# Five modulation blocks moved out of the weight ring of a fused two-block transformer kernel

## The reference, cut to what matters

```python
for l in range(DEPTH):                      # first block, DEPTH = 2, x is 256 x 1024
    x = layer_norm(ALPHA * x + 0.5 * swiglu(x, ffn_w1[l, 0], ffn_w2[l, 0]), ...)
    x = layer_norm(ALPHA * x + hybrid_mixer(x, ...), ...)
    x = layer_norm(ALPHA * x + 0.5 * swiglu(x, ffn_w1[l, 1], ffn_w2[l, 1]), ...)

def adaln(cond, w_mod, b_mod):              # second block, for c and c_ctx
    m = silu(cond) @ w_mod + b_mod          # 1024 x 3072 a layer
    return split(m)                         # shift, scale, gain
...
for layer in range(DEPTH):
    h = rms_norm(x, g_pre) * (1 + scale) + shift        # latent and context rows
    y = even_mixer(h) if layer == 0 else odd_mixer(h)
    x = x + gain * rms_norm(y, g_post)
```

## Time and profile before

| | |
|---|---|
| median of 3 runs | 2401.09 us (2400.11 to 2401.63) |
| the profiled execution | 2397.17 us, span 2395.4 us |
| mean granted TensorE clock | 0.975 |
| PE busy | 94% (2252.9 us) |
| DVE busy | 59% |
| ACT busy | 37% |
| mean busy share of 16 DMA engines by q1 | 38.1% |

### The profile page before, as it was taken

One profiled execution on the slowest core, in us unless ns is written; L12 is line 12 of the kernel. 1 busy time (PEld: TensorE's weight loads), 2 busy tenths in 40 slices (PEclk: granted clock), 3 DMA queues, 4 the chain that ended last, 5 costly groups with the idle time before them and its releaser, 6 DMA issues.

```text
span 2395.4 us, 34326 instructions
## 1 busy us (share of the span) xinstructions
PE 2252.9 (94%) x14514; PEld 1966.8 (82%) x14514; DVE 1409.0 (59%) x2025; ACT 878.2 (37%) x993; POOL 10.5 (0%) x23
## 2 busy tenths in 40 slices
PE   7997999899979979999998989999999998999988
PEld 7985999699869959998897658888777757999966
DVE  5554876655455547766655546665655348565663
ACT  4432364143324323552432242222334242343432
POOL 0000000000000000000000000000000000000000
PEclk9998999999989989999999999999999998999998
DMA  6454555455454545555554511111101242232321
GB/s 257 181 205 164 192 196 181 171 197 208 176 193 178 208 166 189 193 182 206 200 208 151 193 71 70 71 71 71 71 36 71 79 175 72 80 132 76 137 106 53
DMA packets 26552, 349.39 MB, mean 146 GB/s; under 512 B 2912, under 2 KB 3168, under 8 KB 5728
## 3 DMA queue, kind: packets, MB, share of 16 engines
q1 hardware_dynamic: 23888, 336.49, 38.1%
q0 software_dynamic: 2512, 10.72, 1.3%
HBM read 346.14 MB, written 1.05 MB: 145 GB/s over the span
## 4 chain that ended last, share of the span: by engine, by line
PE 85%; DVE 6%; ACT 3%; DMA 3%; DVEq 1%; issue 1%; ACTq 1%; SPq 0%
PE banks L695 12%; PE banks L700 12%; PE banks L696 12%; PE banks L778 10%; PE banks L854 8%; PE banks L916 5%; PE banks L912 5%; PE banks L913 5%; DMA ring<-weights 2%; PE banks L737 2%; PE banks L1091 2%; PE banks L1092 2%; DVE w_lo L1784 2%; PE banks L1089 2%; PE banks L930 2%; PE banks L926 2%
## 5 line engine op out<-in xcount | busy, mean ns | idle before, releaser
L1784 DVE TENSOR_TENSOR w_lo<-ring,w_hi 128x2048 fp32r<-128x2048 f32 x290 | 662.5, 2291 | 537.3 <-ACT w_hi L1294 533.9
L1294 ACT ACTIVATE w_hi<-ring 128x2048 fp32r<-128x2048 f32 x290 | 554.8, 1916 | 766.7 <-PE banks L700 476.7
L695 PE MATMUL banks<-x_hi,w_hi 128*128 128x256 f32 x2208 | 515.0, 276 | 1.4 <-ACT arena L1388 1.4
L696 PE MATMUL banks<-x_lo,w_hi 128*128 128x256 f32 x2208 | 514.2, 276 | 0.0
L695 PEld LDWEIGHTS banks<-x_hi,w_hi 128*128 128x128 f32 x2208 | 414.4, 188 | 1.8 <-ACT arena L1388 1.8
L696 PEld LDWEIGHTS banks<-x_lo,w_hi 128*128 128x128 f32 x2208 | 414.4, 188 | 0.0
L700 PE MATMUL banks<-x_hi,w_lo 128*128 128x256 f32 x2208 | 295.4, 276 | 0.0
L700 PEld LDWEIGHTS banks<-x_hi,w_lo 128*128 128x128 f32 x2208 | 270.8, 188 | 0.4 <-DVE w_lo L1784 0.4
L1325 ACT ACTIVATE arena<-banks 128x512 f32<-128x512 f32 (+3 forms) x164 | 79.6, 498 | 451.6 <-PE banks L916 196.4
L912 PE MATMUL banks<-x_hi,w_hi 128*128 128x512 f32 (+1 forms) x656 | 239.5, 376 | 3.9 <-DVEq L2355 3.9
L913 PE MATMUL banks<-x_lo,w_hi 128*128 128x512 f32 (+1 forms) x656 | 230.7, 363 | 0.0
(11 more groups left out here) (316 smaller groups left out, 2779.1 us busy)
## 6 DMA issues: line engine op xcount, KB each, us to landing
ring<-weights SPq DMA_DIRECT2D x159, 2048.0 KB, 7.7
bcast<-lnrows POOLq DMA_DIRECT2D x12, 512.0 KB, 9.6
arena<-hy_consts POOLq DMA_DIRECT2D x1, 1152.0 KB, 13.5
xrow<-x SPq DMA_DIRECT2D x1, 1024.0 KB, 5.1
arena<-hy_consts POOLq DMA_DIRECT2D x1, 1024.0 KB, 15.5
xrow<-ctx_rows POOLq DMA_DIRECT2D x1, 1024.0 KB, 5.2
out<-xrow SPq DMA_DIRECT2D x2, 512.0 KB, 2.7
filt_sb<-filt POOLq DMA_DIRECT2D x1, 609.0 KB, 11.6
```

The costliest lines, as they stand in the source:

```text
L695: nc.tensor.matmul(out, hi[:, k, t * P:(t + 1) * P], x_h[:, k, :], start=k == 0, stop=False)
L696: nc.tensor.matmul(out, hi[:, k, t * P:(t + 1) * P], x_l[:, k, :], start=False, stop=False)
L1294: nc.scalar.activation(hi, raw, ACT.Copy).then_inc(w_hi_done, 1)
L1784: v.tensor_tensor(lo, raw, hi.bitcast(F32), ALU.subtract).then_inc(w_lo_done, 1)
```

## The change

Modulation blocks 0 to 4 leave the ring and the input `weights`. They are a new input `mods`, loaded one after the other into one buffer `mod_w` in the arena (it lies over `th_g`). SP issues these loads behind the ring loads of certain blocks. The filter's inputs lie elsewhere and are loaded earlier, behind the use of modulation block 4; `f_sum`, `f_dif` and `f_mag` change places. The first even block is split behind `pre`. `gif` takes bank 3. In the last head `mod_row(11)` goes to where the next head's queries would be, the first output half follows the head's products, the rows' banks change, and `mt_split` comes in three pieces.

```diff
@@ layer_blocks
-    last = mod(5, 6, 7) if l == DEPTH - 1 else mod(3 * l + 2)
-    return up(0) + down(0) + mod(3 * l) + mix + mod(3 * l + 1) + up(1) + down(1) + last
+    return up(0) + down(0) + mix + up(1) + down(1) + (mod(5, 6, 7) if l == DEPTH - 1 else [])
@@ plan_banks
-                           ... ("gif", 0),
+                           ... ("gif", 3),
-        "odd_y": (1, in_turn(*[("y", r, h, 4 + 2 * r + h) for r in range(RT) for h in range(2)])),
+        "odd_y": (1, in_turn(*[("y", r, h, 4 * h + r) for r in range(RT) for h in range(2)])),
@@ build
+        mod_w = arena[:, top[0]:top[0] + BLK].rearrange("p (k n) -> p k n", k=KT)
-        top[0] = heads_at + 3 * D
-        f_sum = part(2 * D, 2, D)
+        filt_sb = place("filt_sb", [P, FILTCOLS], F32, arena_at + 4 * top[0])
+        f_mag = part(2 * D, 2, D)
-        filt_sb = place("filt_sb", [P, FILTCOLS], F32, xt_at)
-        f_dif = place("f_dif", [P, 2, D], F32, xt_at)
-        f_mag = place("f_mag", [P, 2, D], F32, xt_at + 8 * D)
+        f_sum = place("f_sum", [P, 2, D], F32, xt_at)
+        f_dif = place("f_dif", [P, 2, D], F32, xt_at + 8 * D)
@@ SP, behind the ring load of block n
+                l, kind, *rest = block_keys[n]
+                if l < DEPTH and (kind, *rest) in (("down", 0, 0), ("up", 1, 0), ("down", 1, 0)):
+                    m = 3 * l + (("down", 0, 0), ("up", 1, 0), ("down", 1, 0)).index((kind, *rest))
+                    if m >= 5:
+                        continue
+                    if m:
+                        filled(sp, *mod_key("mrow", m - 1))
+                    if kind == "up":
+                        sp.wait_ge(m_done, 4 * l + 4)
+                    sp.dma_start(mod_w, mods[m].rearrange("p (k n) -> p k n", k=KT)).then_inc(S2["mod_in"], 16)
@@ POOL
+                        filled(pool, *mod_key("mrow", 4))
                         pool.dma_start(hyw[:], hy_consts[:, 0:HYW]).then_inc(S2["hy_in"], 16)
...
-                        filled(pool, l, "layer", "up", 1, FJ - 1, 1)
                         pool.dma_start(filt_sb[0:HY_HIDDEN, :], filt).then_inc(S2["hy_in"], 16)
@@ PE, mod_row
+                if m < 5:
+                    w = mod_w
+                    if ks[0] == 0:
+                        pe.wait_ge(S2["mod_in"], 16 * m + 16)
@@ PE, last head and tail
+                else:
+                    mod_row(11, range(KT))
                 released(pe, i, "ml", "v", 0)
...
                 else:
-                    mod_row(11, range(KT))
+                    odd_half(0, 0)
                 pe.wait_ge(S2["hn_done"], 2 * i + 2)
...
-            for j in range(4):
+            mod_columns(11)
+            odd_half(0, 1)
+            pe.wait_ge(S2["gcol_done"], 2)
+            for h in range(2):
+                gain_rows(take(pe, 0, "tail", "gg", h), 1, 0, h)
+            for j in (1, 2, 3):
                 for side in range(2):
-                    out_half("odd_y", "oy", j, side, ...)
-                    if j == 0 and side == 0:
-                        mod_columns(11)
-                if j == 0: ... gain_rows ...
+                    odd_half(j, side)
@@ ACT, even stage
-            for side in range(2):
-                weights_hi(HALF_OF[DEPTH, "hy", 0, side])
             act.wait_ge(S2["gain_done"], 1)
             pre("even", 0)
-            for m in (6, 7):
-                mod_copy(m)
+            mod_copy(6)
+            for side in range(2):
+                weights_hi(HALF_OF[DEPTH, "hy", 0, side])
+            mod_copy(7)
@@ ACT, last head
+                    copy(mt2_hi[:, 0:4, :], mt2[:, 0:4, :], S2["mt_hi"])
                 after(DEPTH, "oz", i, 1)
+                if i == ML_HEADS - 1:
+                    mod_copy(11)
...
-                    copy(mt2_hi[:, 0:2 * i, :], mt2[:, 0:2 * i, :], S2["mt_hi"])
+                    copy(mt2_hi[:, 4:2 * i, :], mt2[:, 4:2 * i, :], S2["mt_hi"])
...
-            mod_copy(11)
@@ DVE, even stage: both weights_lo of "hy", 0 from ahead of pre to behind pre_split
@@ DVE, last head
+                    mt_split(slice(0, 4), 1)            # behind the decayed scores
-                    mt_split(slice(0, 2 * i), 1)
+                    mt_split(slice(4, 2 * i), 2)
-            mt_split(slice(2 * KT - 2, 2 * KT), 2)
+            mt_split(slice(2 * KT - 2, 2 * KT), 3)
```

More of the change, by code:

```diff
@@ L253, in plan_banks @@
         "odd": (1, in_turn(*[(kind, m, m - 8) for m in (8, 9) for kind in ("mrow", "mcol")],
-                           *[("pre", k, k) for k in range(KT)], ("mrow", 10, 2), ("mcol", 10, 2), ("gif", 0),
+                           *[("pre", k, k) for k in range(KT)], ("mrow", 10, 2), ("mcol", 10, 2), ("gif", 3),
                            ("ct", 6), ("em", 7))),
@@ L268, in plan_banks, with build @@
     return table
-def build(nc, weights, cols, lnrows, consts, cols2, hy_consts, filt, gate_w, ctx_rows, x, out):
+def build(nc, weights, mods, cols, lnrows, consts, cols2, hy_consts, filt, gate_w, ctx_rows, x, out):
     plan = plan_banks()
@@ L728, in mod_row @@
             def mod_row(m, ks):
-                n, key = MOD_BLOCK[m], mod_key("mrow", m)
+                key = mod_key("mrow", m)
+                if m < 5:
[3 more added lines that the diff above has]
+                else:
+                    n = MOD_BLOCK[m]
+                    w = ring[:, n % RING]
+                    pe.wait_ge(wt_in[n % RING], 16 * (n // RING + 1))
                 if ks[0] == 0:
-                    pe.wait_ge(wt_in[n % RING], 16 * (n // RING + 1))
                     take(pe, *key)
@@ L736, in mod_row @@
                 for k in ks:
-                    mm = nc.tensor.matmul(banks[0:2, b, :], cond[:, k, :], ring[:, n % RING, k, :], start=k == 0,
-                                          stop=k == KT - 1)
+                    mm = nc.tensor.matmul(banks[0:2, b, :], cond[:, k, :], w[:, k, :], start=k == 0, stop=k == KT - 1)
                 if ks[-1] == KT - 1:
@@ L1218, in _, with odd_half @@
             mm.then_inc(full[b], 1)
+            def odd_half(j, side):
+                out_half("odd_y", "oy", j, side, mt2_hi, mt2_lo, RT, lambda h, r: (r, h),
+                         lambda k: pe.wait_ge(S2["mt_split"], 1 if k < 4 else 2 if k < 2 * KT - 2 else 3))
             for i in range(ML_HEADS):
@@ L1260, in _ @@
                 mm.then_inc(full[b], 1)
-            for j in range(4):
-                for side in range(2):
-                    out_half("odd_y", "oy", j, side, mt2_hi, mt2_lo, RT, lambda h, r: (r, h),
-                             lambda k: pe.wait_ge(S2["mt_split"], 1 if k < 2 * KT - 2 else 2))
-                    if j == 0 and side == 0:
-                        mod_columns(11)
[L1267 to L1270, removed]
+            mod_columns(11)
[4 more added lines that the diff above has]
+            for j in (1, 2, 3):
+                for side in range(2):
+                    odd_half(j, side)
         @block.scalar
@@ L2080, in _ @@
             prenorm(0, erow)
-            for side in range(2):
-                weights_lo(HALF_OF[DEPTH, "hy", 0, side])
             def pre(seg, layer):
@@ L2099, in _ @@
             pre_split(0)
+            weights_lo(HALF_OF[DEPTH, "hy", 0, 0])
             for p in (3, 4):
@@ L2110, in _ @@
             v.drain().then_inc(S2["conv_done"], 1)
+            weights_lo(HALF_OF[DEPTH, "hy", 0, 1])
             for m in (6, 7):
@@ L2448, in _ @@
                     dve.sem_inc(free[bb], 1)
+                if i == ML_HEADS - 1:
+                    mt_split(slice(0, 4), 1)
                 for side in range(2):
@@ L2527, in weight_blocks @@
         ffn(0)
-        modulation(3 * l)
         w = i["w_in"][l]
@@ L2542, in weight_blocks, with early_modulation @@
         out.extend(units(i["w_o"][l]))
-        modulation(3 * l + 1)
         ffn(1)
-        modulation(*((5, 6, 7) if l == DEPTH - 1 else (3 * l + 2,)))
+    modulation(5, 6, 7)
     return out
+def early_modulation(i):
+    return np.stack([i["w_mod_2"][0][:, 512 * m:512 * (m + 1)].reshape(KT, P, 512).transpose(1, 0, 2).reshape(P, BLK)
+                     for m in range(5)])
 def second_blocks(i):
@@ L2692 @@
         "weights": np.stack(weight_blocks(i) + second_blocks(i)),
+        "mods": early_modulation(i),
         "cols": np.ascontiguousarray(columns(i)),
```

3 lines of the change are left out of this document (2 added, 1 removed).

## The result

The changed kernel takes 2323.39 us (median of 4 runs, 2320.27 to 2325.17), the one before 2400.6 in the same comparison: a ratio of 0.968, 95% interval 0.9664 to 0.9697. That is 77.2 us less, where 85.3 were forecast. The time lies in the forecast's range (2303 to 2337), 7.6 above the 2315.8 that was forecast. The profiled execution took 2325.17 with a span of 2323.4, so between the two profiles lie 72.0 us.

What follows compares the result with a forecast made beforehand. PE, busy nearly throughout, bounds it by work, rests and low clock. 52.2 - 3.7 + 11.0 + 3.2 + 8.6 + 4.9 + 0.6 + 8.5 = 85.3 us off the median 2401.1 gave 2315.8, range 2303 to 2337.

Steps and rivals of the forecast that it cites:

- Waits at stage ends: Five stage ends: 52.2 us of PE's waits for the norm and bank 4 go, less 3.7 for row tile 1.
- Clock of rows and transposes: Five stage ends: transposes gain 0.8 and the modulation row 1.4 each from full clock, 11.0 us in all.
- Clock of the first columns: First 48 column products behind a stage end: full clock gains 1.6 us at two places, 3.2 in all.
- Loads at no cost: Five modulation loads moved beside ring loads: cost 0; at worst a first load lands with the second, 7.7 us late.
- third rival: At `wo`, loads land in pairs, the norm shifts by 4.3 us, PE waits 3.6 twice: 2325 us; chance 0.10.
- Filter: Filter inputs: the 6.4 us wait for `filt_sb` goes, with 2.2 of clock; sum 8.6, bounds 6.4 and 9.
- Even stage: Before `mod_row(6)`: `pre` starts sooner, saving 2.6 us of the 5.13 wait, plus 2.3 of clock; sum 4.9.
- Odd stage: Gate product's new bank frees PE from a 3.9 us wait; gain between 0 and 2.3, taken as 0.6.
- Tail: Last head: `mod_row(11)` moves into a 5.33 us wait and output halves come earlier; gain 8.5, from 6.0 to 10.6.
- first rival: Around stage ends the clock stays at 1.2 GHz through short remaining waits; 21 us lost, 2337 us; chance 0.13.
- second: Rival: at second down and up blocks, modulation loads in SP's queue delay ring loads; 2405 us or more; chance 0.02.
- fourth: Rival: DVE's split isn't what holds the norm, the 52.2 us stay, only 22 are gained: 2379 us; chance 0.02.

Runs made afterwards that it cites:

- order_only: Kernel before, ring untouched, with only DVE's last low split ahead of each norm put behind it: 2351.98 us, ratio 0.979.
- mods_only: Kernel before with only modulation blocks 0 to 4 taken out of the ring: 2345.22 us, ratio 0.974.
- Filler: Changed kernel plus twelve transposes with unused results on PE behind each stage end's transposes: 2326.64 us, ratio 0.966 to the kernel before.
- late: Changed kernel with three modulation loads put behind the last down block's ring load instead of the first's: 2325.58 us, ratio 0.968 to the kernel before.
- odd_order: Changed kernel with the low split of the first `oz` half ahead of DVE's logarithm: 2334.07 us, ratio 0.969 to the kernel before.
- no_tail: Changed kernel with the last head and output products as before the change: 2338.53 us, ratio 0.973 to the kernel before.
- no_filt: Changed kernel with the filter's inputs loaded late again, in their old place: 2335.26 us, ratio 0.972 to the kernel before.
- no_even: Changed kernel with both halves of the first even block split ahead of `pre` again: 2330.92 us, ratio 0.971 to the kernel before.

## Why the prediction was right, and where it was off

The mechanism held at the stage ends, which carry 59.2 of the 72.0: a modulation block's place in the ring made the load late, the load the splits, and the low split the norm. order_only shows the middle link alone, mods_only the first.

- **Waits at stage ends.** 52.2 of the earlier trace rows less a residual of 3.7 were forecast; the row for `xrow` fell from 48.8 to 3.2, in four pieces of up to 1.0, and the 3.4 for L1809 left. The arithmetic of the next load's landing (7.84 from 185.87, low split done at 197.97 where 196.9 was forecast) was good to about 1 us.
- **Clock of rows and transposes.** 11.0 forecast. Every half row of the five ends is 3.59 or 3.60 now, the transposes 1.09 and, behind the short wait, 1.32.
- **Clock of the first columns: this term failed.** The prediction counted "1.6 for the columns twice", a gain of 3.2. They take 33.6 in all, where the kernel before had 31.9: a loss of 1.7, and so a miss of 4.9. The prediction named the wait for tile 1's transposes and not the one behind it, for `x_lo`, which the kernel before had too (8.9 us in five pieces) and which the earlier trace rows left out. It called the waits that remain short, on the strength of one row that ran at full clock after a rest of 2.63. That row was no safe witness: `mod_row(10)` behind the same rest took 7.03 in eight profiles and 8.4 to 8.6 in six, the changed kernel's among them. Filler shows that the rest is the cause, by keeping PE occupied there. The rests of the five ends fell from 61.0 to 10.8 in all, 50.2 where 48.5 were forecast, and rows and transposes gave 10.7 by difference. So E gave 59.2 where 62.7 (52.2 - 3.7 + 11.0 + 3.2) were forecast.
- **Loads at no cost.** Right. The products of the down projection wait 2.1 once for `w_lo` in the changed kernel, and as long in the kernel before, where the blocks are still in the ring; late shows that the place of the loads doesn't matter. A modulation load takes 9.8 to 13.1 from issue to landing, and nothing waits for it. The third rival's pairs don't appear: the ring loads issued just before and just after the five modulation loads take 7.6 to 8.1.
- **Filter.** 8.6 forecast, 7.4 and 8.1 measured.
- **Even stage: right by luck.** 4.9 forecast, 5.3 between the two profiles. The wait gave 2.5 of the 2.6 forecast. The clock term of 2.3 gave 1.1: behind the rest of 2.63 both rows took 15.34, and in no profile the 14 that was forecast, so this rest isn't free either. The 1.7 that made up for it is the spectra's clock, which goes with the group and not with the change; within one group the part is 3.0 to 3.5.
- **Odd stage.** The prediction said that "PE then only arrives earlier at a point where DVE's gate chain sets the time", which is what happened, and took a gain of 0.6, with 0 as its lower bound. The runs show a loss: in O 0.2 to 0.6 in one group (964.9 against 965.1 to 965.5) and 2.7 to 3.1 in the other (963.0 against 965.7 to 966.1), from one profile each with the old bank. The bound was wrong: ACT's copies, for which DVE waits, came later and not sooner. That they stand behind PE's new 6.8 us wait fits the rows, but odd_order, which took that wait away, didn't bring them forward.
- **Tail.** 8.5 forecast, 6 to 8 by no_tail and the three profiles with the old tail, 8.0 between no_tail and the changed kernel. From the start of `mod_row(11)` to the end of the second output half it takes 32.7 (2277.85 - 2245.17); the kernel before took 41.1 from the start of the head's rest at 2308.75 to 2349.8. The first output half takes 5.8, at full clock but for its start; the second takes 7.5, inside the 5.5 to 8.55 that were allowed for it.
- **Together.** O gained 6.6 where 9.1 (0.6 and 8.5) were forecast. The four stretches that the change touches and S gained 77.6, 7.7 below the forecast: 3.5 at stage ends, 1.2 in the filter, 2.5 in O, 0.9 in S, less 0.4 in V.
- **What it said the profile would show.** The wait for L1846 "under 2 in total" is 3.2, the mean clock 0.987 and not 0.99, and the load is still in the chain at two of the five stage ends (185.87 and 822.52). Both rows behind the rest of `mod_row(6)` take 15.3 and not 14. The wait before the first scores is 5.7 as before, and not longer: PE spent the time in the new wait at L944, which the prediction didn't have. The rest is as it said.

The first rival (the clock stays down) is seen in small, at three stage ends and behind the rest ahead of `mod_row(6)`. The second, third and fourth didn't come.

## What to carry to other kernels

When a wait names one producer, follow the chain back on that producer's own engine: a queue in order can be held by a piece of work that has nothing to do with the data waited for. Either taking away what makes that piece late or putting it behind the critical one cures it, and one of the two is enough. After a large wait has gone, list the small ones right behind it: here a rest of 1.7 us brought the clock down in 23 of 32 places. An engine freed ahead of a chain on another engine only arrives sooner at its next wait. And before a part of a few us is read off two profiles, see whether work that no edit touched took the same time in both.

## What the runs showed of the hardware

**Two paces at the same granted clock.** The same products without a wait, at a granted clock of 1.00, ran at one of two rates. Windows of PE in the same stretch (busy, count, granted clock, DMA share, GB/s), of the changed kernel and of odd_order:

```profile
490.00:510.00 20.00, 20.00 (x172) 1.00 0.44 158
```

```profile
490.00:510.00 20.00, 20.00 (x179) 1.00 0.51 198
```

172 against 179 in 20 us is 4%. Of the four stretches of P the second and third took 175.8 or 181.4, the first and fourth 226.5 or 230.4, each within 0.6 and with nothing in between. The longer time came in 7, 5, 5 and 4 of the profiles, in order of the stretches, and it went with no edit: all of P came to 804.5 at best (filler) and 820.0 at worst (no_filt and no_even, which change nothing there). S has two levels as well, 200.6 to 202.2 and 206.2 to 208.2, and so has F, where mods_only, no_even and odd_order counted 172 products in 20 us and the changed kernel 179. The changed kernel's own profile had one such stretch and that of the kernel before none, which is the 5.5 in P. The scatter between runs of one kernel is of this size too. What sets the pace wasn't tried and stays open, as does what puts a profile into one or the other of the two groups that no_even's section describes; the share of the DMA engines doesn't order it, since it is lower in the slower of these two windows (0.44 against 0.51) and higher in another pair, from 550 to 570 us (0.59 against 0.52), at the same counts.
